# Moving state space constants beside a projection block and loading rows untransformed, in a one-core decoder step

## The chip, the cores and the metric

The kernel runs on one core of a Trainium2 chip. The metric is device time in microseconds (us). Three timed runs stand before the change, and beside them one profiled execution, from which every row below comes.

## The reference, cut to what matters

One inference step of one decoder layer in float32, for 1024 prompt rows and 32 sample rows (8 samples of 4) of width 1024:

```
z  = rmsnorm(x, norm_mix) @ w_in                # [q | k | v | u], 3*768 + 256 columns
q, k = rope(rmsnorm(q)) / 8, rope(rmsnorm(k))   # 12 heads of 64 in 3 groups
attn = dilated window attention of (128,1), (512,4), (2048,16), mixed by a softmax over the groups' lse
y  = S5 state space: a = exp(lam*dt), b = c*B u, h_t = a h_(t-1) + b_t, y = Re(C h) + D u; GLU on gelu(y)
h  = x + [rmsnorm(attn) | rmsnorm(ssm)] @ w_out
h  = h + cross attention(rmsnorm(h), 256 memory rows; sample rows against cached rows) @ w_xo
out = h + ConvFFN(rmsnorm(h))
```

rmsnorm(x, g) is x * rsqrt(mean(x*x) + 1e-6) * g, so the factor of a row and the gain of a column may each be applied to either side of the product with w_in.

## The kernel before

Each product runs as three float32r products (high*high, high*low, low*high) of matrices split into XH, XL (rows, transposed, 128 a tile) and WH, WL (weights, 256 columns a block). ScalarE writes the high half, VectorE subtracts to get the low half. Four stretches follow one another, each a block whose five queues (SyncE for DMA, GpSimd, ScalarE, VectorE, TensorE) are written out by hand; within a queue the order is fixed, between queues there are semaphores.

**block_project** walks 81 steps s: blocks b = 0 to 8 of w_in (for each head group in turn q, k, v; block 2 takes u beside v and is 512 wide), in each the row tiles t = 0 to 8 (tile 8 has 32 rows). In block 0 the rows are made ready too. `prepare(i)` on ScalarE squares and sums tile i (L343) and forms Ln then Exp (L333, L334); on VectorE it refines the root (L89 to L92) and multiplies the tile by factor and gain (L441); TensorE transposes it (L549), ScalarE copies XH (L351), VectorE XL (L448). A step is 24 matmuls (L629), an evacuation by ScalarE (L405, L407), and for q and k blocks a chain for the per-head norm: GpSimd squares (L307), VectorE sums (L458), ScalarE Ln and Exp one step later (L333, L334), GpSimd scales (L286 to L295), VectorE gain and rotation (L466 to L476), TensorE transposes two steps on (L560), ScalarE copies q or k (L383). At the block's start ScalarE asks once for the activation table set `natural_log_exp_and_others` (L327), which has both functions.

Attention of tile a is spread over four steps: scores (L576), mask and maximum on VectorE (L486, L493), exponentials on ScalarE (L363), transposes of the probabilities (L590), their copies on ScalarE (L371) and, where there are 256 keys, on VectorE (L501), the product with V (L605), and the scaling of the result (L509). In a step VectorE does `take_output`, `mask_and_max`, `take_probabilities` in this order. The group with 256 keys in nearly every tile runs beside block 8.

Weights go through one buffer, wstage: SyncE loads it when the split before it is done; ScalarE splits in four pieces of 128x512 (L322), VectorE too (L433).

**block_middle** does the state space layer, the sample rows' attention over cached rows (28 pairs of key tiles, each transposed at L1350 and multiplied at L1363, loads by SyncE into ring slots), and brings everything into XH, XL for the output product. VectorE begins with constants from lam and dt (L1086 to L1135, with two Sin on ScalarE at L952, L953), then the input weights (WBR, WBI), the output table CA; GpSimd doubles a table of unit powers ER, EI from 1 to 128 columns (L870 to L875), then multiplies U by D (L897). VectorE's scans (L1185 to L1202) wait for that table. The Toeplitz parts follow (L1447, DMA to TZ, L1457), y (L1473, L1477), the sample softmax (L1230 to L1245), the mixing weights of the groups (L1254 to L1279), the gates (L1525), and 36 pieces of transposes (L1560) with a high half on ScalarE (L1051) and a low half on VectorE (L1318). The first block of w_out is split in between (L1064, L1333).

**block_dense** multiplies by w_out, the memory weights and w_xq; **block_cross** is cross attention in 16 units, with 64 cached tiles of the samples loaded into an 8-slot ring; the first block of w_xo is split in its unit 14 (L2116, L2186). Then block_dense by w_xo, and the ConvFFN, which the change leaves alone.

Of the kernel before, what the change touches and what calls it, by code (L numbers as in the profile page):

```python
# [13 lines left out]
P = 128  # L14
# [85 lines left out]
def block_project(nc, I, O, S):  # L100
# [12 lines left out]
    MM, TR, SC, OB = bank[0:3], bank[3:5], bank[5:7], bank[7]  # L113
    BLOCKS = 9
# [5 lines left out]
    with ExitStack() as c:  # L120
# [6 lines left out]
        ssq = sb("ssq", [P, 3, TILES])  # L127
        zs = sb("zs", [P, 3, GW])
# [12 lines left out]
        x_ld = [sem(f"x_ld{i}") for i in range(2)]  # L141
        x_sq = sem("x_sq")
        x_rt = sem("x_rt")
        x_n = sem("x_n")
# [29 lines left out]
        zero = sem("zero")  # L174

# [27 lines left out]

        def due(s, after):

            return [a for a in range(G * NT) if start[a] + after == s]
# [17 lines left out]
        def _(sp):  # L224
# [5 lines left out]

            for i in range(TILES):
                if i >= 2:
                    sp.wait_ge(x_tr, 2 * (i - 1))
                src = I["x_prompt"][0, P * i:P * i + P, :] if i < NT else \
                    I["x_sample"].rearrange("b t d -> (b t) d")
                sp.dma_start(xin[:rows(i), i % 2, :], src).then_inc(x_ld[i % 2], 16)
# [5 lines left out]
            lamR, lamI, dt_, Bin = S["ssm_in"]  # L242
# [11 lines left out]
            for s in range(BLOCKS * TILES + 1):  # L254
                b, t = s // TILES, s % TILES
                if s - 1 in k_step:
# [19 lines left out]
        def _(pool):  # L276
            nc.gpsimd.memset(S["eps"][:], EPS).then_inc(zero, 1)
            link = linker(pool, c_pool)

            def scale(q):  # L280
# [4 lines left out]
                sums, r, tmp = (zr[:n, x, q] for x in range(3))  # L285
# [5 lines left out]
                if q >= 4:  # L291
                    pool.wait_ge(z_tr, q - 3)
                    if k_stores[q]:
# [3 lines left out]
                                        per_head(zr[:n, 1, q], n), ALU.mult).then_inc(z_s, 1)  # L297

            for s in range(BLOCKS * TILES):
# [9 lines left out]
                if s in norm_at:  # L309
                    scale(norm_at[s])  # L310

# [4 lines left out]
        def split_weights_act(act, n):  # L316
# [3 lines left out]
            for x in range(CHUNKS):  # L320
                ks = slice(KC * x, KC * x + KC)
                nc.scalar.activation(WH[:, n % 2, ks], wstage[:, ks], ACT.Copy).then_inc(w_hi, 1)  # L322

        @blk.scalar
        def _(act):
# [10 lines left out]
            def prepare(i):  # L336

                if i < TILES:
                    n = rows(i)
                    act.wait_ge(x_ld[i % 2], 16 * (i // 2 + 1))  # L340
                    if i:
                        act.wait_ge(x_sq, i)
                    nc.scalar.activation(junk[:n], xin[:n, i % 2], ACT.Square,  # L343
                                         accum_out=ssq[:n, 0, i:i + 1]).then_inc(x_sq, 1)
                    act.wait_ge(x_sq, i + 1)
                    rsqrt_of_mean(ssq[:n, 0, i:i + 1], ssq[:n, 1, i:i + 1], D).then_inc(x_rt, 1)
                if 0 < i <= TILES:
                    n = rows(i - 1)
                    for half in range(2):
                        act.wait_ge(x_tr, 2 * (i - 1) + half + 1)  # L350
                        nc.scalar.activation(XH[:, 4 * half:4 * half + 4, P * (i - 1):P * (i - 1) + n],  # L351
                                             TR[half][:, 0:4 * P].rearrange("p (k n) -> p k n", k=4)[:, :, :n],
                                             ACT.Copy).then_inc(x_hi, 1)
            prepare(0)
            prepare(1)
            split_weights_act(act, 0)

# [26 lines left out]

            for s in range(LAST):
                b, t = s // TILES, s % TILES
                turn, kind, n = b // 3, b % 3, rows(t)
                if b == 0:
                    prepare(t + 2)
                if b < BLOCKS:  # L390
# [12 lines left out]
                    act.wait_ge(mm, s + 1)  # L403
                    if b == PAIR:
                        nc.scalar.activation(U[:, :, t] if t < NT else US[:, :].rearrange("p (g h) -> p g h", g=16),  # L405
                                             MM[s % 3][:n, WB:2 * WB].rearrange("p (g h) -> p g h", g=16), ACT.Copy)
                    nc.scalar.activation(dst, src, ACT.Copy).then_inc(ev, 1)  # L407
                    if s in take_at:
                        take_q_or_k(take_at[s])
                    if s in norm_at:  # L410
# [3 lines left out]
                        rsqrt_of_mean(zr[:n_q, 0, q], zr[:n_q, 1, q], E).then_inc(z_rt, 1)  # L414
# [9 lines left out]
        def _(dve):  # L424
            link = linker(dve, c_dve)
            dve.wait_ge(tab, 16 * len(S["tables"]))
            link(nc.vector.tensor_scalar(qk_gain[:, 0], qk_gain[:, 0], E ** -0.5, None, ALU.mult))

            def split_weights(n):
                for x in range(CHUNKS):  # L430
                    ks = slice(KC * x, KC * x + KC)
                    dve.wait_ge(w_hi, CHUNKS * n + x + 1)
                    nc.vector.tensor_tensor(WL[:, n % 2, ks], wstage[:, ks], WH[:, n % 2, ks].bitcast(F32),  # L433
                                            ALU.subtract).then_inc(w_lo, 1)

            def prepare(i):
                if i < TILES:
                    n = rows(i)
                    dve.wait_ge(x_rt, i + 1)
# [3 lines left out]
                if 0 < i <= TILES:  # L443
                    n = rows(i - 1)
                    for half in range(2):
                        dve.wait_ge(x_hi, 2 * (i - 1) + half + 1)
                        ks, ts = slice(4 * half, 4 * half + 4), slice(P * (i - 1), P * (i - 1) + n)
                        nc.vector.tensor_tensor(XL[:, ks, ts],  # L448
                                                TR[half][:, 0:4 * P].rearrange("p (k n) -> p k n", k=4)[:, :, :n],
                                                XH[:, ks, ts].bitcast(F32), ALU.subtract).then_inc(x_lo, 1)  # L450
            prepare(0)
            prepare(1)
            split_weights(0)

            def sum_squares(q):
                n = rows(QK[q][1])
                dve.wait_ge(z_sq, q + 1)
                nc.vector.tensor_reduce(zr[:n, 0, q], zsq[:n, q % 2].rearrange("p (h e) -> p h e", h=H),  # L458
# [45 lines left out]
            def take_output(a):  # L504
# [3 lines left out]
                dve.wait_ge(at_pv, a + 1)  # L508
                nc.vector.tensor_tensor(att[:, at].rearrange("p (h e) -> p h e", h=H),  # L509
                                        OB[:, 0:GW].rearrange("p (h e) -> p h e", h=H),  # L510
                                        per_head(rl[:, at], P), ALU.mult).then_inc(at_o, 1)

            for s in range(LAST):
                b, t = s // TILES, s % TILES
                if b == 0:
                    prepare(t + 2)
# [15 lines left out]
        def _(pe):  # L532
# [7 lines left out]
            pe.wait_ge(tab, 16 * len(S["tables"]))  # L540

            def transpose_x(i):
                n = rows(i)
                pe.wait_ge(x_n, i + 1)
# [2362 lines left out]
```

## Time and profile before

| | us |
|---|---|
| three timed runs | 1947.91, 1943.61, 1944.77 |
| median | 1944.77 |
| the profiled execution, its own time | 1944.68 |
| its span, first to last instruction | 1942.8 |
| TensorE busy in the span | 1792.9 (92%) |
| VectorE, ScalarE, GpSimd busy | 960.4, 665.6, 249.0 |
| mean granted clock | 0.962 |

The profiled execution lies 0.1 us from the median, and 1.9 us of it lie outside its span. TensorE's idle time is 150 us. A busy TensorE isn't one at full speed: the granted clock has two levels, 1.2 and 2.4 GHz, and the mean granted clock tells how much of a stretch was at the higher one.

### The profile page before, as it was taken

Reading aid. Unit: us, or ns where it says so; the run is one execution under the profiler, and the core shown is the slowest. Engines: PE = TensorE matmul, PEld = TensorE weight load, DVE = VectorE, ACT = ScalarE, POOL = GpSimd, SP = SyncE. Lnnn points to the kernel's source line nnn. Section 1 sums busy time; section 2 is a strip of 40 time slices with the busy share of each in tenths; the row PEclk is TensorE's granted clock in tenths of the full one; section 3 lists DMA queues with packets and bytes.
Section 4 is the critical chain, followed back from the end, with each engine's and each line's share of the span. In section 5 each row is a group of like instructions: output and inputs, shape, how many; then the busy total and the mean of one; then the engine's idle time right before and its main releaser. Section 6 shows DMA issues by size and latency. Waiting matters only on the chain. (4 is left out here: it accounts for less than half of the span.)

```text
span 1942.8 us, 31346 instructions
## 1 busy us (share of the span) xinstructions
PE 1792.9 (92%) x12419; PEld 1633.8 (84%) x12419; DVE 960.4 (49%) x1929; ACT 665.6 (34%) x1559; POOL 249.0 (13%) x566
## 2 busy tenths in 40 slices
PE   5889999998586998999999989999999999999998
PEld 5888998986354998898678979899899899889996
DVE  5523524646556534653353264545555454454545
ACT  5424324444155323543432054233223223223230
POOL 1511611608221000000000000000000000000000
PEclk9999999998786999999999989999999999999999
DMA  4210110005242532200642112111211112112102
GB/s 151 61 47 32 47 39 26 4 5 158 47 144 85 196 97 77 77 23 27 197 127 74 44 34 56 54 47 34 65 33 56 43 33 66 33 33 66 32 23 90
DMA packets 136239, 125.66 MB, mean 65 GB/s; under 512 B 15722, under 2 KB 128434, under 8 KB 136116
## 3 DMA queue, kind: packets, MB, share of 16 engines
q1 hardware_dynamic: 130500, 109.74, 18.4%
q0 software_dynamic: 5632, 14.44, 2.3%
q8 instruction: 74, 1.21, 0.3%
q14 instruction: 33, 0.27, 0.0%
HBM read 112.79 MB, written 10.70 MB: 64 GB/s over the span
## 5 line engine op out<-in xcount | busy, mean ns | idle before, releaser
L2649 PE MATMUL bank<-XH,WH 128*128 128x352 f32 x1056 | 344.4, 326 | 1.0 <-PEq L1612 1.0
L2649 PE MATMUL bank<-XH,WL 128*128 128x352 f32 x1056 | 342.0, 324 | 0.0
L2649 PE MATMUL bank<-XL,WH 128*128 128x352 f32 x1056 | 341.1, 323 | 0.0
L1969 PE MATMUL bank<-WH,XH 128*128 128x256 f32 x768 | 223.9, 292 | 12.4 <-DVE WL L1836 7.4
L1969 PE MATMUL bank<-WL,XH 128*128 128x256 f32 x768 | 219.5, 286 | 0.0
L629 PE MATMUL bank<-WH,XH 128*128 128x256 f32 (+3 forms) x648 | 212.2, 328 | 7.7 <-DVE WL L433 7.7
L1969 PE MATMUL bank<-WH,XL 128*128 128x256 f32 x768 | 218.5, 285 | 0.0
L2557 DVE TENSOR_TENSOR hres<-hres,bank 128x512 f32<-128x512 f32 (+2 forms) x198 | 135.7, 686 | 158.2 <-PE bank L2682 158.2
L629 PE MATMUL bank<-WL,XH 128*128 128x256 f32 (+3 forms) x648 | 203.7, 314 | 0.0
L629 PE MATMUL bank<-WH,XL 128*128 128x256 f32 (+3 forms) x648 | 203.3, 314 | 0.0
L2649 PEld LDWEIGHTS bank<-XH,WH 128*128 128x128 f32 x1056 | 199.5, 189 | 2.7 <-issue 1.1
L2649 PEld LDWEIGHTS bank<-XL,WH 128*128 128x128 f32 x1056 | 200.0, 189 | 0.4
L2649 PEld LDWEIGHTS bank<-XH,WL 128*128 128x128 f32 x1056 | 199.3, 189 | 0.0
L1969 PEld LDWEIGHTS bank<-WH,XH 128*128 128x128 f32 x768 | 148.4, 193 | 14.0 <-DVE WL L1836 8.1
L2513 DVE SCALAR_TENSOR_TENSOR cv<-UB,pT,cv 128x1072 f32<-128x1072 f32 x44 | 58.7, 1334 | 191.9 <-ACT cv L2460 191.9
L629 PEld LDWEIGHTS bank<-WH,XH 128*128 128x128 f32 (+1 forms) x648 | 139.8, 216 | 11.0 <-issue 8.8
L1969 PEld LDWEIGHTS bank<-WH,XL 128*128 128x128 f32 x768 | 148.6, 193 | 0.0
L1969 PEld LDWEIGHTS bank<-WL,XH 128*128 128x128 f32 x768 | 148.5, 193 | 0.0
L629 PEld LDWEIGHTS bank<-WL,XH 128*128 128x128 f32 (+1 forms) x648 | 140.3, 216 | 1.5
L629 PEld LDWEIGHTS bank<-WH,XL 128*128 128x128 f32 (+1 forms) x648 | 139.6, 215 | 1.7
L2451 ACT ACTIVATE UB<-bank 128x352 f32<-128x352 f32 x88 | 36.1, 463 | 281.0 <-PE bank L2649 281.0
L2682 PE MATMUL bank<-DH,AH 128*128 128x512 f32 x320 | 127.2, 398 | 1.4 <-DVE hres L2557 1.4
(494 smaller groups left out, 3260.0 us busy)
## 6 DMA issues: line engine op xcount, KB each, us to landing
wstage<-w_up SPq DMA_DIRECT2D x44, 512.0 KB, 5.3
ring<-cache_mem_kv SPq DMA_DIRECT2D x64, 256.0 KB, 3.8
dstage<-w_down POOLq DMA_DIRECT2D x22, 512.0 KB, 3.8
wstage<-w_in SPq DMA_DIRECT2D x10, 1024.0 KB, 5.3
ringS<-cache_kv_dil SPq DMA_DIRECT2D x16, 512.0 KB, 6.4
wstage<-w_xkv SPq DMA_DIRECT2D x8, 1024.0 KB, 5.8
ringS<-cache_kv_dil SPq DMA_DIRECT2D x48, 128.0 KB, 2.8
xin<-x_prompt SPq DMA_DIRECT2D x8, 512.0 KB, 3.5
```

The costliest lines, as they stand in the source:

```text
L629: ins = nc.tensor.matmul(out, x, w[:, :, k] if pair else w[:, load % 2, k], start=k == 0 and j == 0, stop=k == KT - 1 and j == 2)
L1969: ins = nc.tensor.matmul(MM[s % 3][:r, 0:WB], x[:, k, cols], w[:, b % 2, k], start=k == 0 and i == 0, stop=k == KT - 1 and i == 2)
L2451: nc.scalar.activation(UB[:, g, 2 + CH * j:2 + CH * j + CH], bank[3 * g + j][:, 0:CH], ACT.Copy)
L2513: nc.vector.scalar_tensor_tensor(cv[:, g], UB[:, g, 1:W - 1], taps(slot, 17, g), cv[:, g], ALU.mult, ALU.add).then_inc(c_dve, 1)
L2557: nc.vector.tensor_tensor(dst, dst, bank[6 + u % 2][:r], ALU.add).then_inc(y, 1)
L2649: ins = nc.tensor.matmul(bank[3 * g + j][:, 0:CH], w[:, slot, k, P * g:P * g + P], x[:, k, CH * j:CH * j + CH], start=k == 0 and i == 0, s ...
L2682: ins = nc.tensor.matmul(out[:r, :], x, w[:, cols], start=s == 0 and i == 0, stop=s == 1 and i == len(terms) - 1)
```

## The change

It has four places.

Start of block_project: the rows are transposed as loaded (three buffers for them rather than two, the first weights asked for before the other tables). The gain of the norm goes into the weights, as the scale of ScalarE's split and as the scalar of VectorE's, now eight pieces of 128x256 each. The factor of a row goes into the evacuation, as a per-partition scale; for the v blocks of the dilated groups it is brought into their order through a small DRAM tensor.

State space constants: the whole of their computation stands in block 2 of block_project, Exp and Sin included, and the table of unit powers up to 64 columns on GpSimd; block_middle does the last doubling.

Order: in block_project `take_probabilities` comes ahead of `mask_and_max` on VectorE. In block_middle the weights' transposes come earlier, keys are divided otherwise (0-2, 2-4, 4-6, 6-16, 16-24, 24-28), the three sums of squares stand after the scans, the first four pieces of the last part are taken ahead of the root, and GpSimd makes the low half of the first w_out block.

block_cross: the second half of the cached tiles uses 12 slots (the four of kTx too), and the split of w_xo's first block moves from unit 14 to behind unit 15.

```diff
@@ block_project
-        zr = sb("zr", [P, 3, len(QK), H])
+        zr = sb("zr", [P, 3, 8, H])
-            xin = early.enter_context(nc.sbuf_tensor("xin", [P, 2, D], F32))
+            xin = early.enter_context(nc.sbuf_tensor("xin", [P, XB, D], F32))      # XB = 3
+        def row_factor(s):
+            b, t = s // TILES, s % TILES
+            order = GROUPS[b // 3] if b % 3 == 2 and t < NT else 0
+            return (r_dil[:, order - 1] if order else ssq[:, 1])[:rows(t), t:t + 1]
@@ sync
+            sp.dma_start(S["ident"][:], I["c_ident"]).then_inc(id_ld, 16)
             for i in range(TILES):
-                if i >= 2:
-                    sp.wait_ge(x_tr, 2 * (i - 1))
+                if i >= XB:
+                    sp.wait_ge(x_tr, 2 * (i - XB + 1))
+                    sp.wait_ge(x_sq, i - XB + 1)
...
                 if i == 0:
+                    sp.dma_start(gain[:], I["norm_mix"][0].rearrange("(k p) -> p k", p=P),
+                                 allow_slow_non_contiguous=True).then_inc(g_ld, 16)
+                    load_weights(0)
+                if i == 2:
                     for dst, src in S["tables"]:
                         sp.dma_start(dst, src).then_inc(tab, 16)
-                if i in (1, 4):
-                    load_weights(i // 4)
+                if i == 4:
+                    load_weights(1)
...
+                if (b, t) == (1, 1):
+                    sp.wait_ge(x_r, TILES)
+                    (store ssq[:, 1] to rowf, wait, load r_dil twice)
@@ gpsimd
+                if (b, t) == (PAIR, 3):
+                    unit_powers()                # 3 squarings, then doubling from 1 to 64 columns
@@ scalar
-            for x in range(CHUNKS):
-                ks = slice(KC * x, KC * x + KC)
-                nc.scalar.activation(WH[:, n % 2, ks], wstage[:, ks], ACT.Copy).then_inc(w_hi, 1)
+            for k in range(KT):
+                ins = nc.scalar.activation(WH[:, n % 2, k], wstage[:, k], ACT.Copy, scale=gain[:, k:k + 1])
+                if k % KC == KC - 1:
+                    ins.then_inc(w_hi, 1)
...
+            take_rows(0)
+            act.wait_ge(g_ld, 16)
             split_weights_act(act, 0)
+            mean_square(0)
...
+            def step_sizes():
+                act.wait_ge(S["ld_lam"], S["n_lam"])
+                nc.scalar.activation(dt_[:], dt_[:], ACT.Exp).then_inc(p_dt, 1)
+            def magnitude_and_angle():
+                act.wait_ge(p_exp, 1)
+                nc.scalar.activation(sm[:, 1], sm[:, 0], ACT.Exp).then_inc(p_exp, 1)
+                act.wait_ge(p_ang, 1)
+                nc.scalar.activation(sm[:, 16], sm[:, 5], ACT.Sin).then_inc(p_sin, 1)
+                nc.scalar.activation(sm[:, 17], sm[:, 4], ACT.Sin).then_inc(p_sin, 1)
             for s in range(LAST):
                 b, t = s // TILES, s % TILES
-                if b == 0:
-                    prepare(t + 2)
+                if (b, t) == (PAIR, 0):
+                    step_sizes()
+                if (b, t) == (PAIR, 2):
+                    magnitude_and_angle()
+                if b == 0 and t < NT:
+                    take_rows(t + 1)
...
+                    if b == 0:
+                        act.wait_ge(x_r, t + 1)
+                    if s == 2 * TILES:
+                        act.wait_ge(r_ld, 32)
-                    nc.scalar.activation(dst, src, ACT.Copy).then_inc(ev, 1)
+                    nc.scalar.activation(dst, src, ACT.Copy, scale=row_factor(s)).then_inc(ev, 1)
...
+                if b == 0 and t < NT:
+                    mean_square(t + 1)
@@ vector
-                    refine_rsqrt(nc, link, ssq[:n, 0, i:i + 1], ssq[:n, 1, i:i + 1], ssq[:n, 2, i:i + 1], D)
-                    nc.vector.scalar_tensor_tensor(xin[:n, i % 2], xin[:n, i % 2], ssq[:n, 1, i:i + 1],
-                                                   gain_bc[:n], ALU.mult, ALU.mult).then_inc(x_n, 1)
...
                 if b == 0:
-                    prepare(t + 2)
+                    finish_factor(t)             # the four small operations of refine_rsqrt
+                    if t < NT:
+                        take_rest(t + 1)         # XL
+                if (b, t) == (PAIR, 1):
+                    decay_and_angle()
+                if (b, t) == (PAIR, 3):
+                    powers()
+                if (b, t) == (PAIR, 5):
+                    input_weights()
...
                 for a in due(s, 3):
                     take_output(a)
+                for a in due(s, 2):
+                    take_probabilities(a)
                 for a in due(s, 0):
                     mask_and_max(a)
-                for a in due(s, 2):
-                    take_probabilities(a)
@@ block_middle
 sync
-            load_ring(0, 3)
+            load_ring(0, 2)
...
+            load_ring(RING, 8)
+            sp.wait_ge(e_tab, 1)
             sp.dma_start(gain_bc[:, 0:AW], I["attn_out_norm"][0].partition_broadcast(P)).then_inc(ld_g, 16)
             sp.dma_start(gain_bc[:, AW:D], I["ssm_out_norm"][0].partition_broadcast(P)).then_inc(ld_g, 16)
-            load_ring(RING, 20)
+            load_ring(8, 18)
             sp.wait_ge(tz, 4)
...
-            load_ring(20, 24 + RING)
+            load_ring(18, 24 + RING)
 gpsimd
-            (3 squarings of the unit step, then doubling of ER, EI from 1 to 128 columns)
+            (8 operations on 128x512: ER, EI [0:64] copied, [64:128] made from them, scratch in CA) -> e_tab
...
+            pool.wait_ge(S["w_first_hi"], 1)
+            nc.gpsimd.tensor_tensor(S["WL"][:, 0], S["wstage"][:], S["WH"][:, 0].bitcast(F32), ALU.subtract)\
+                .then_inc(S["w_first"], 1)
 scalar
             nc.scalar.preload_act_table_set("natural_log_exp_and_others")
-            act.wait_ge(ld_lam, S["n_lam"])
-            nc.scalar.activation(dt_[:], dt_[:], ACT.Exp).then_inc(p_dt, 1)
             nc.scalar.activation(st[:, :, 0], lsum[:], ACT.Ln).then_inc(lnp, 1)
-            (Exp, Sin, Sin)
...
-            take_keys(22, KPAIRS)
+            squares(1)
+            take_keys(24, KPAIRS)
+            squares(2)
 vector
-            (decay and angle, powers, input weights: L1086 to L1135)
...
             dve.wait_ge(t_c, 1)
+            dve.wait_ge(e_tab, 1)
...
-            sum_squares(0)                       # ahead of the scans
...
-            sum_squares(1)
-            sum_squares(2)
+            for g in range(G):
+                sum_squares(g)
...
+            for k in range(EARLY):               # 4, ahead of the root
+                take_rest(k)
             dve.wait_ge(so_r, 1)
...
-            nc.vector.tensor_tensor(S["WL"][:, 0], S["wstage"][:], S["WH"][:, 0].bitcast(F32), ALU.subtract)\
-                .then_inc(S["w_first"], 1)
@@ block_cross
-    slot = [n % RING if n < 2 * NL - LATE else 4 + n % 4 for n in range(2 * NL)]
+    WIDE = RING + SLOTS
+    slot = [n % RING if n < NL else (n - NL) % WIDE for n in range(2 * NL)]
...
-                if v == NU - 2:
-                    act.wait_ge(S["w_next"], 32)
-                    act.wait_ge(vp, NL - LATE)
-                    nc.scalar.activation(WH[:, 0], wstage[:], ACT.Copy).then_inc(S["x_hi"], 1)
             act.wait_ge(vp, NL)
             nc.scalar.activation(Ps[:], SB[:, 2 * P:4 * P], ACT.Copy).then_inc(so_c, 1)
+            act.wait_ge(S["w_next"], 32)
+            nc.scalar.activation(WH[:, 0], wstage[:], ACT.Copy).then_inc(S["x_hi"], 1)
             take_output(NU - 1)
```

## Rows read from the trace of the kernel before

**Rows 1.** The page's part 2: TensorE and its granted clock in 40 slices.

```profile
PE   5889999998586998999999989999999999999998
...
PEclk9999999998786999999999989999999999999999
```

**Rows 2.** TensorE's waits, 0 to 480 us: waited for, total us, times, longest.

```profile
PE bank L549 <- DVE xin L441: 13.3, 1, 13.3
...
PE bank L605 <- DVE PT L501: 6.6, 6, 2.7
```

**Rows 3.** TensorE's waits, 470 to 640 us, same columns.

```profile
PE bank L1447 <- DVE R L1188: 16.3, 1, 16.3
PE bank L1560 <- DVE XL L1318: 14.0, 6, 10.2
PE bank L1457 <- DMA TZ<-R: 7.0, 1, 7.0
```

**Rows 4.** Stretches of the span: length, busy us and instructions of each engine, clock.

```profile
core 0: us, PE busy (x) PEld busy (x) DVE busy (x) ACT busy (x) POOL busy (x), PEclk, DMA share, GB/s
18.34:73.97 55.63, 43.06 (x287) 40.00 (x285) 35.71 (x96) 27.88 (x75) 17.47 (x50) 0.88 0.32 91
...
206.96:244.39 37.43, 37.17 (x315) 36.40 (x314) 21.96 (x71) 14.74 (x52) 29.42 (x84) 1.00 0.11 36
341.35:372.57 31.22, 31.08 (x263) 30.52 (x262) 18.72 (x60) 12.61 (x44) 24.31 (x70) 1.00 0.00 1
401.41:430.97 29.56, 26.43 (x220) 24.40 (x218) 14.85 (x24) 11.77 (x41) 0.00 (x0) 1.00 0.01 1
439.55:624.47 184.92, 125.11 (x1527) 84.74 (x1525) 118.60 (x269) 84.80 (x180) 70.54 (x98) 0.79 0.37 103
```

**Rows 5.** Timeline at the start: start us, us, instruction; and the page's weight loads.

```profile
4.76 0.43 SPq L228 DMA_DIRECT2D wstage<-w_in  x1
...
18.34 0.56 PE L629 MATMUL bank<-WH,XH 128*128 128x256 f32 x1
...
wstage<-w_in SPq DMA_DIRECT2D x10, 1024.0 KB, 5.3
```

**Rows 6.** VectorE's groups, 0 to 75 us: busy us, mean ns, idle before.

```profile
L441 DVE SCALAR_TENSOR_TENSOR xin<-xin,ssq,gain_bc 128x1024 f32<-128x1024 f32 (+1 forms) x9 | 11.9, 1327 | 0.3
```

**Rows 7.** Timeline of ScalarE in one step of block 3.

```profile
210.18 0.39 ACT L407 ACTIVATE zs<-bank 128x256 f32<-128x256 f32 x1 [1.99 <-PE bank L629]
210.46 0.38 ACT L383 ACTIVATE qT<-bank 128x256 f32<-128x256 f32 x1
210.72 0.30 ACT L333 ACTIVATE zr<-zr,eps 128x4 f32<-128x4 f32 x1
211.05 0.21 ACT L334 ACTIVATE zr<-zr 128x4 f32<-128x4 f32 x1
```

**Rows 8.** Timeline of ScalarE in the middle: table loads and what follows them.

```profile
444.13 1.28 ACT L952 ACT_TABLE_LOAD   x1
...
546.68 1.28 ACT L999 ACT_TABLE_LOAD   x1
547.97 0.21 ACT L999 ACTIVATE sc<-sc 128x3 f32<-128x3 f32 x1
548.20 1.28 ACT L1001 ACT_TABLE_LOAD   x1
...
561.32 1.28 ACT L1012 ACT_TABLE_LOAD   x1
```

**Rows 9.** Timeline of VectorE in the middle's first half.

```profile
443.70 0.17 DVE L1086 TENSOR_TENSOR sm<-lamR,dt_ 128x8 f32<-128x8 f32 x1 [0.32 <-ACT dt_ L947]
...
454.77 1.23 DVE L1073 TENSOR_TENSOR WBR<-PR,BpR 128x1024 f32<-128x1024 f32 x1
...
484.36 0.69 DVE L1185 TENSOR_TENSOR XR<-ER,bank 128x512 f32<-128x512 f32 x1 [9.04 <-POOL EI L875]
...
488.85 2.83 DVE L1073 TENSOR_TENSOR XI<-XI,R 128x512 f32<-128x512 f32 x1
```

**Rows 10.** Timeline of GpSimd there: last doubling's operations, then U by D.

```profile
481.82 1.28 POOL L874 TENSOR_TENSOR ER<-XR 128x512 f32<-128x512 f32 x1
...
486.02 5.11 POOL L897 TENSOR_TENSOR U<-U,Dbc 128x1024 f32<-128x1024 f32 x2
```

**Rows 11.** Timeline of ScalarE and VectorE at the middle's last part.

```profile
596.46 1.15 ACT L1051 ACTIVATE XH<-bank 128x256 fp32r<-128x256 f32 x4
...
600.58 1.40 DVE L1318 TENSOR_TENSOR XL<-bank,XH 128x256 fp32r<-128x256 f32 x4
614.06 2.28 DVE L1333 TENSOR_TENSOR WL<-wstage,WH 128x2048 fp32r<-128x2048 f32 x1
```

**Rows 12.** TensorE's waits, 640 us to the end.

```profile
PE bank L2259 <- DMA ring<-cache_mem_kv: 2.3, 1, 2.3
PE bank L2224 <- DVE PT L2144: 2.2, 2, 1.6
```

More of the change, by code:

```diff
@@ L127, in block_project @@
         ssq = sb("ssq", [P, 3, TILES])
+        r_dil = sb("r_dil", [P, 2, NT])
+        gain = sb("gain", [P, KT])
         zs = sb("zs", [P, 3, GW])
@@ L139, in block_project @@
         PT = sb("PT", [P, 2, 2 * H, P])
-        x_ld = [sem(f"x_ld{i}") for i in range(2)]
+        x_ld = [sem(f"x_ld{i}") for i in range(XB)]
         x_sq = sem("x_sq")
         x_rt = sem("x_rt")
-        x_n = sem("x_n")
+        x_r = sem("x_r")
+        r_st, r_ld = sem("r_st"), sem("r_ld")
+        id_ld, g_ld = sem("id_ld"), sem("g_ld")
         x_tr = sem("x_tr")
@@ L283, in scale @@
                 pool.wait_ge(z_rt, q + 1)
-                sums, r, tmp = (zr[:n, x, q] for x in range(3))
+                sums, r, tmp = (zr[:n, x, q % 8] for x in range(3))
                 link(nc.gpsimd.tensor_scalar(tmp, sums, -0.5 / E, -0.5 * EPS, ALU.mult, ALU.add))
@@ L425, in _, with split_weights @@
             link = linker(dve, c_dve)
+            def split_weights(n):
+                for x in range(CHUNKS):
+                    dve.wait_ge(w_hi, CHUNKS * n + x + 1)
+                    for k in range(KC * x, KC * x + KC):
+                        ins = nc.vector.scalar_tensor_tensor(WL[:, n % 2, k], wstage[:, k], gain[:, k:k + 1],
+                                                             WH[:, n % 2, k].bitcast(F32), ALU.mult, ALU.subtract)
+                    ins.then_inc(w_lo, 1)
@@ new lines, in take_rest @@
+            def take_rest(i):
+                n = rows(i)
+                for half in range(2):
+                    dve.wait_ge(x_hi, 2 * i + half + 1)
+                    ks, ts = slice(4 * half, 4 * half + 4), slice(P * i, P * i + n)
+                    nc.vector.tensor_tensor(XL[:, ks, ts],
+                                            TR[half][:, 0:4 * P].rearrange("p (k n) -> p k n", k=4)[:, :, :n],
+                                            XH[:, ks, ts].bitcast(F32), ALU.subtract).then_inc(x_lo, 1)
@@ new lines, in finish_factor @@
+            def finish_factor(i):
+                n = rows(i)
+                dve.wait_ge(x_rt, i + 1)
+                sums, r, tmp = (ssq[:n, x, i:i + 1] for x in range(3))
+                link(nc.vector.tensor_scalar(tmp, sums, -0.5 / D, -0.5 * EPS, ALU.mult, ALU.add))
+                link(nc.vector.tensor_tensor(tmp, tmp, r, ALU.mult))
+                link(nc.vector.tensor_tensor(tmp, tmp, r, ALU.mult))
+                nc.vector.scalar_tensor_tensor(r, tmp, 1.5, r, ALU.add, ALU.mult).then_inc(x_r, 1)
@@ L426, in _ @@
+            take_rest(0)
+            dve.wait_ge(g_ld, 16)
+            split_weights(0)
             dve.wait_ge(tab, 16 * len(S["tables"]))
             link(nc.vector.tensor_scalar(qk_gain[:, 0], qk_gain[:, 0], E ** -0.5, None, ALU.mult))
[L429 to L434, printed above, removed]
@@ L964, in _, with take_weights @@
             take_u(3)
-            squares(0)
-            take_keys(0, 4)
+            take_keys(0, 2)
+            def take_weights(q):
+                act.wait_ge(t_b, q + 1)
+                nc.scalar.activation((WBR, WBI)[q // 2][:, 4 * (q % 2):4 * (q % 2) + 4],
+                                     QB[q][:].rearrange("p (g n) -> p g n", g=4), ACT.Copy).then_inc(wb, 1)
+            for q in range(3):
+                take_weights(q)
+            take_keys(2, 4)
             act.wait_ge(us_p, 1)
@@ L1064, in _ @@
             nc.scalar.activation(S["WH"][:, 0], S["wstage"][:], ACT.Copy).then_inc(S["w_first_hi"], 1)
-            for k in range(22, len(work)):
+            for k in range(23, len(work)):
                 take_head(k)
@@ L1204, in _ @@
                     dve.wait_ge(h_ok, 1)
-            sum_squares(1)
-            sum_squares(2)
+            for g in range(G):
+                sum_squares(g)
             dve.wait_ge(s_rd, 3)
@@ L1304, in _, with take_rest @@
                     .then_inc(so_m, 1)
+            def take_rest(k):
+                dve.wait_ge(x_h, k + 1)
+                dst, n = place(XL, work[k])
+                hi, _ = place(XH, work[k])
+                src = mix_bank(k)[:, 0:2 * P].rearrange("p (k n) -> p k n", k=2)[:, :, :n]
+                nc.vector.tensor_tensor(dst, src, hi.bitcast(F32), ALU.subtract).then_inc(x_l, 1)
+            for k in range(EARLY):
+                take_rest(k)
             dve.wait_ge(so_r, 1)
@@ L1401, in _, with transpose_weights @@
             transpose_u(3)
-            keys(0, 4)
+            keys(0, 2)
+            def transpose_weights(q):
+                for g in range(4):
+                    ins = nc.tensor.transpose(QB[q][:, P * g:P * g + P], (WBR, WBI)[q // 2][:, 4 * (q % 2) + g], ident[:])
+                ins.then_inc(t_b, 1)
+            pe.wait_ge(u_t, 4)
+            pe.wait_ge(bb, 1)
+            for q in range(3):
+                transpose_weights(q)
+            keys(2, 4)
             pe.wait_ge(ld_us, 16 * DT)
@@ L2012, in block_cross @@
         ss = sb("ss6", [P, 4])
-        r_ld = [sem(f"r_ld{i}") for i in range(RING)]
+        r_ld = [sem(f"r_ld{i}") for i in range(WIDE)]
         zero, qz = sem("zero"), sem("qz")
@@ L2030, in filled, with cached @@
             return x.rearrange("p b (h n) -> p b h n", h=X)[:, :, :, 0:DT]
+        def cached(n):
+            return ring[:, slot[n]] if slot[n] < RING else kTx[:, slot[n] - RING]
         def out_place(Xt, u):
```

375 lines of the change are left out of this document (189 added, 186 removed).

## The prediction, made before the changed kernel was run

> **What bounds the kernel now.** I read the 40 slices first [rows 1]. TensorE is at 8 or 9 tenths nearly everywhere; the holes are the first slice (5) and the 10th to 13th (8, 5, 8, 6), which are the middle, and the clock row dips only in these four. So the kernel is bound by TensorE, which idles 150 us of 1942.8: 18.3 before the first product [rows 5], 12.6 between 18.34 and 73.97 (block 0) and 59.8 in the middle [rows 4]. In the norm steps 33 to 44 TensorE is all but full, 37.17 of 37.43 us, and ScalarE has 14.74; in 60 to 69 it is 31.08 of 31.22 and 12.61 [rows 4]. Then TensorE's waits by releaser: the head waits for the first normalised tile (13.3), attention for VectorE's copy of PT (6.6 in six) [rows 2]; the middle for the scans' R (16.3), for XL (14.0) and for TZ (7.0) [rows 3]; later parts for the ring (2.3) and PT (2.2) [rows 12]. A gain must come from these waits; a loss needs an engine that passes TensorE.
>
> **Head.** Removed: nine L441 on VectorE, 11.9 us [rows 6], and the path norm, then transpose. The transposes need only a loaded tile, so the 13.3 us wait [rows 2] is replaced by one for the weights. They are asked for at 4.76 [rows 5], eighth on SyncE's queue; now fourth, four issues of 0.43 earlier (-2), and nothing of tables or broadcast gain (0.5 MB) goes ahead of their 1 MB: 5.3 us to landing by the page's row, where 18.34 - 4.76 leaves 13.6 for landing and split. Landing near 8, first quarter split and copied (about 2), transposes and tile copies beside it: first matmul at about 12.5, -5.8 (bounds -2, the issues alone, and -8). After it block 0 is a chain of ScalarE, GpSimd and VectorE: 55.6 us for nine steps, 6.2 each, TensorE busy 43.1 [rows 4]. Of the 1.33 us that leave VectorE per step half lies on that chain (bounds: none, all): 9 x 0.66 = -6. Added: ScalarE scales by a pointer. No row has a Copy with one; L333 with its bias pointer takes 0.30 beside L334 without, 0.21 [rows 7]: 0 to 0.09 each, I take 0.09. Eight split pieces for four cost about +0.8 on ScalarE, and each evacuation waits for the row's factor (x_r), behind which stand Ln and Exp of the chain: +3 together in block 0. Head: -9 (-4 to -13). The store and two loads for r_dil are on SyncE at step 10 and needed at step 18; behind them queue only stores of k, eight steps ahead of use. Nothing.
>
> **Constants in block 2.** Steps there are 512 columns wide, twice a norm step's 3.10 us of TensorE, and have no norm: VectorE's chain of 443.70 to 454.77, 11 us [rows 9], is spread over six steps, and GpSimd's small operations too lie beside 6.2 us of products a step. Cost 0; without that cover, 11.
>
> **Order of VectorE.** PT ahead of mask and maximum takes VectorE's mask work off the path to L605. The waits listed are 6.6 us [rows 2]; mask and maximum stand ahead of PT in each of them, and explain those in block 8 and part of the other two. I take -5.5, bounds 0 and -8.2 (with L560's).
>
> **Middle.** The path was: 11 us of constants, table doubled on GpSimd until 484.3, scans from 484.36 after 9.04 us of idle VectorE [rows 9], and then VectorE slowed beside GpSimd's L897 (128x512 in 2.83 against 0.69 [rows 9, 10]). Now eight operations of 128x512 at 1.28 [rows 10] are 10.2 us, so it is there by 460 even if they start ten us into the middle, and the scans start when their products are there: these wait for transposes and keys that TensorE has in its order ahead of them, near 475 as I place it (-9; bounds 0 and -19, from 484.36 to 465, VectorE's constants gone and nothing else late), and run some 3.5 faster. L1447's 16.3 wait [rows 3] is filled with keys, which are only moved, so the gain is the part of it that TensorE can't fill again later. TZ's 7.0 goes too, since the TZ stores no longer queue on SyncE behind ring loads up to 19. Against: SyncE waits for e_tab, and the gain rows and eleven ring loads stand behind it (ring tiles late by about 5 us); three sums and squares stand ahead of the sample softmax, +5 to 6 on its chain. Tail: four pieces ahead of the root take 4 us of XL's 14.0 [rows 3], and WL (2.28 on VectorE [rows 11]) goes to GpSimd: 2048 columns by L897's 5.11 for 2 x 1024 [rows 10] are 5.1 us, needed only after the last transposes, so hidden; if it slows VectorE's 0.35 us pieces [rows 11] as L897 did, +4. With Sin gone from the middle the set asked for at its start stays: the loads at L952, L999, L1001 and L1012 [rows 8] go, two of them off the softmax (-2.6), which then waits for its DMA round trip. Together -18: 13 of scans, TZ and softmax, 5 of tail; bounds -6 (tail and one wait) and -24.
>
> **Cross.** Twelve slots remove the ring wait, 2.3, and about 1.5 of half-clock products behind it; PT's 2.2 goes [rows 12]. The split of w_xo now stands after the last unit: ScalarE and VectorE need some 2 us each there, hidden in part by take_output: +1.5. Sum -4.5 (0 to -6).
>
> **Table loads.** This is the step that costs. Block 2 now calls Sin at step 20, after the one request for the joint Ln and Exp set (L327). While that set is in, a norm is Ln and Exp with no load between [rows 7]. After a Sin the trace of before shows otherwise: L999 loads 1.28 us for Ln, the next instruction begins 0.01 later, and then L1001 loads 1.28 again for Exp [rows 8]. The same would hold for the 36 norms after step 20: 72 loads, 92 us of ScalarE. Blocks 3, 4, 6 and 7 with no attention give 23 pure steps (33 to 44, 60 to 70). ScalarE there has 14.74 / 12 = 1.23 us, 1.05 counting overlap [rows 4, 7]; with 2.56 of loads, 0.09 to 0.18 of pointers and 0.1 of waits about 3.9, against TensorE's 37.17 / 12 = 3.10. So ScalarE sets these steps: +0.8 x 23 = +18. Two of them also split weights (+3 each, +6); the four norm steps with attention, whose steps are longer, +3; +1 of clock. Sum +28. Ends: 0 (no loads) and +56 (rival B).
>
> A rule stands beside it. The Trainium skill, "ScalarE: Activation LUTs", section "What ACT_TABLE_LOAD costs", gives a load about 1283 ns and a drain of about 1380 ns after it. The row's 1.28 agrees; the 0.01 us that follow L999's load do not [rows 8]. By the page's drain the sum would have 72 x 1.38 = 99 us more; by the row, none.
>
> **Sum.** -9 - 5.5 - 18 - 4.5 + 28 = -9. The profiled execution took 1944.68, 0.1 under the median: 1936.
>
> **Rivals.** *A, the joint set comes back.* If what follows Sin is one load of the joint set, or the set of Ln holds Exp, one load is hidden in block 2 and the other four gains stay: 1944.7 - 37 = 1908. For: the request's name is a set with both, and [rows 7] run on it. Against: [rows 8], where Exp right after Ln loads again. A sentence of the Trainium skill speaks for it ("ScalarE: Activation LUTs", section on table sets): ln then exp is one load, since natural_log_exp_and_others has both; rows 8 contradict it, and by it the time is this rival's.
>
> *B, slower: the clock follows the idle.* In the steps bound by ScalarE TensorE idles 0.8 of 3.9 us. If its clock falls to the lower level there, 24 matmuls that take 3.10 at the higher one take up to 6.2, and about 5.1 with the weight loads that overlap: 1.2 above the 3.9, x 23 = +28 more: 1964. It decides where the mean clock of steps 33 to 44 goes below about 0.8. For: in block 0, 12.6 idle of 55.6 goes with 0.88, in the middle 0.79. Against: in 401.41 to 430.97 TensorE idles 3.13 of 29.56 in gaps under a microsecond at clock 1.00 [rows 4].
>
> *C, the middle gives little.* If the cache tiles' DMAs bound the middle, and not the scans (DMA share 0.37 [rows 4], and SyncE now stops for e_tab), the waits come back as waits for ring tiles, and the softmax, 5 us later, takes the tail's gain: middle -6, 1948. For: 16.3 us of wait is filled with keys that must come 12 us sooner. Against: no wait of TensorE for ring tiles among the large ones now [rows 3].
>
> **How the numbers follow.** Forecast 0.50, own range 1926 to 1946 (each gain at its lower half to its upper, table loads 20 to 34); A 0.14; B 0.20; C 0.16. A measurement tells about 0.2%, 3.9 us, from no change. Faster (below 1940.9): of the forecast 0.37, A 0.14, of C 0.02: 0.53. Same: 0.09 of the forecast, 0.08 of C, 0.02 of B: 0.19. Slower: the rest, 0.28. The range goes from A to just short of B's middle: 1908 to 1962; outside remain half of A and half of B.
>
> **What would show it.** The first L629 at 12 to 13 and no VectorE operation of 1.33 us in block 0. No VectorE idle for EI, scans from about 475, L1447's wait under 5. No load at the middle's Ln or Exp; L605's wait for PT under 2; L2259's for the ring gone. ScalarE's groups: 72 table loads between steps 28 and 72, steps 33 to 44 in 46 to 48 us rather than 37.4, TensorE waiting there for the evacuation. Wrong would be: one load after Sin, or none (A); steps 33 to 44 above 55 at a clock under 0.8 (B); a wait for ring tiles of over 8 us in the middle (C); or ScalarE's time under 3.1 a step for another reason, such as a norm without its own loads.

## The result and the profile after

| | before | after |
|---|---|---|
| median of 4 runs, us | 1946.03 | 1964.01 (1962.04 to 1969.19) |
| ratio, 95% interval | | 1.0093 [1.0076, 1.0110] |
| span of the profiled execution | 1942.8 | 1962.5 |
| ScalarE busy | 665.6 | 774.6 |
| mean granted clock | 0.962 | 0.954 |

The change made the kernel 0.9% slower where 0.4% faster was forecast. TensorE's row and its clock in the 40 slices of the changed kernel's page, beside [rows 1]: the first slice is fuller, there are new holes in the 4th, 5th, 8th and 9th, and the clock dips in the 8th and 9th too.

```profile
PE   6898799879867889899898989999999999999998
...
PEclk9999999889787899999999989999999999999999
```

ScalarE's groups in the changed kernel (line, operation, count | busy us, mean ns | idle before): behind the two Sin, while TensorE is at steps 28 to 73, the Ln of a norm (L402) and its Exp (L403) each bring a load of an activation table, 72 in all, 92.4 us.

```profile
L402 ACT ACT_TABLE_LOAD x36 | 46.2, 1283 | 0.6
L403 ACT ACT_TABLE_LOAD x36 | 46.2, 1283 | 0.6
...
L402 ACT ACTIVATE zr<-zr,eps 128x4 f32<-128x4 f32 (+1 forms) x54 | 15.9, 294 | 2.7 <-DVE zr L553 2.3
```

Where the time went in the two traces. A step of block_project begins with its first product, and so does each later stretch, with two exceptions: the middle is counted from the end of the last product by w_in, and the stretch to the ConvFFN from the end of cross attention's last product.

| stretch | before | after | difference |
|---|---|---|---|
| to step 0 | 18.3 | 12.9 | -5.4 |
| steps 0 to 8 | 55.6 | 50.7 | -4.9 |
| steps 9 to 26 | 101.1 | 104.7 | +3.6 |
| 27 to 32 (attention) | 31.9 | 37.2 | +5.3 |
| 33 to 44 | 37.4 | 51.2 | +13.8 |
| 45 to 54 | 67.7 | 66.7 | -1.0 |
| 55 to 59 (attention) | 29.3 | 37.9 | +8.6 |
| 60 to 69 | 31.2 | 42.3 | +11.0 |
| 70 to 74 (attention) | 28.8 | 38.5 | +9.6 |
| 75 to 80 (attention, no norm) | 38.1 | 34.0 | -4.1 |
| middle | 184.9 | 172.1 | -12.8 |
| products to cross attention | 293.4 | 293.0 | -0.3 |
| cross attention | 117.4 | 112.4 | -4.9 |
| to the ConvFFN | 121.2 | 123.8 | +2.6 |
| ConvFFN and end | 786.5 | 785.1 | -1.4 |

Five of these stretches as windows of the changed kernel (columns as in [rows 4]): steps 0 to 8, steps 33 to 44, 60 to 69, 75 to 80, middle.

```profile
12.95:63.64 50.69, 40.02 (x286) 37.34 (x285) 27.81 (x99) 32.90 (x89) 16.14 (x50) 0.90 0.35 98
...
205.49:256.69 51.20, 41.05 (x315) 38.74 (x314) 23.31 (x75) 48.49 (x81) 24.93 (x79) 0.93 0.07 24
...
361.28:403.54 42.26, 33.84 (x264) 31.95 (x261) 19.78 (x63) 40.78 (x68) 20.70 (x66) 0.96 0.00 1
...
442.01:476.02 34.01, 34.01 (x293) 32.47 (x292) 16.80 (x29) 13.88 (x43) 0.00 (x0) 1.00 0.02 6
476.02:648.16 172.14, 131.44 (x1525) 90.24 (x1525) 110.92 (x213) 77.32 (x170) 54.66 (x47) 0.77 0.40 111
```

In steps 33 to 44 and 60 to 69 ScalarE is busy 48.49 of 51.20 us and 40.78 of 42.26: the bound has moved to it, where [rows 4] had 14.74 of 37.43. The timeline of one such step, beside [rows 7], has a load ahead of each function (last row: the next step's first load begins 3.76 us after this one's):

```profile
221.90 1.28 ACT L402 ACT_TABLE_LOAD   x1
223.20 0.30 ACT L402 ACTIVATE zr<-zr,eps 32x4 f32<-32x4 f32 x1
223.51 1.28 ACT L403 ACT_TABLE_LOAD   x1
224.80 0.20 ACT L403 ACTIVATE zr<-zr 32x4 f32<-32x4 f32 x1
224.92 0.45 ACT L497 ACTIVATE zs<-bank,ssq 128x256 f32<-128x256 f32 x1
225.27 0.37 ACT L453 ACTIVATE qT<-bank 128x256 f32<-128x256 f32 x1
225.66 1.28 ACT L402 ACT_TABLE_LOAD   x1
```

### The profile page after: what moved, and what is told of

It reads as the page before. It is cut to its first block and busy times, and to the rows that moved or that the text cites. A ratio compares the mean times of both kernels' runs of the same rounds, so it can differ in the third digit from the quotient of the medians.

```text
span 1962.5 us, 31508 instructions
## 1 busy us (share of the span) xinstructions
PE 1810.8 (92%) x12419; PEld 1647.8 (84%) x12419; DVE 958.2 (49%) x1959; ACT 774.6 (39%) x1667; POOL 238.4 (12%) x569
## 3 DMA queue, kind: packets, MB, share of 16 engines
q1 hardware_dynamic: 133620, 109.23, 18.3%
```

## The experiments

The kernel before was timed again beside each group of experiments (median 1948.48 beside E1 to E4, 1948.28 beside E5 to E8, 1943.03 beside E9 and E10, and 1946.03 beside the changed kernel). Across groups the medians can be some us apart for this reason alone, so the difference by the ratios to the kernel before is given too, as us of 1946.

**E1: the joint set asked for again.** The changed kernel with one line, after the two Sin:

```diff
                 nc.scalar.activation(sm[:, 17], sm[:, 4], ACT.Sin).then_inc(p_sin, 1)
+                nc.scalar.preload_act_table_set("natural_log_exp_and_others")
```

> The changed kernel with one more line: right after its two Sin in block 2 ScalarE asks again for the joint set of Ln and Exp. Theory L (the loss is the 72 table loads, by all they set off): the stretches from the first step of block 3 to the end of block 7 give back what they lost, 24.9 us in the steps without attention and 24.8 in those with it; ScalarE shows no load between steps 28 and 72; about 1964 - 49 = 1915. Theory P (part of that loss is something else: evacuations scaled by a pointer, splits in eight pieces, banks held longer): only the forecast's +28 goes, 1936, and steps 33 to 44 stay above 38 us.

Measured 1916.22 us, ratio 0.9836 [0.9822, 0.9850]: 47.8 us under the changed kernel (50 by the ratios), for one added load. ScalarE's groups of this kernel show single loads in block_project, for the request at the start, for Sin and for the request behind it:

```profile
L396 ACT ACT_TABLE_LOAD x1 | 1.3, 1283 | 1.0 <-PEq L3013 1.0
L463 ACT ACT_TABLE_LOAD x1 | 1.3, 1283 | 0.0
L465 ACT ACT_TABLE_LOAD x1 | 1.3, 1283 | 0.0
```

Its windows of steps 33 to 44 and of the middle (the profiled execution of E1 is the fastest of its five, 4.9 under their median, so its trace flatters it a little):

```profile
199.46:237.37 37.91, 37.27 (x315) 36.42 (x314) 23.95 (x81) 16.79 (x56) 28.75 (x83) 1.00 0.10 33
427.97:593.36 165.39, 124.70 (x1525) 83.88 (x1525) 109.84 (x213) 77.25 (x170) 54.72 (x47) 0.82 0.42 115
```

Against the changed kernel the five stretches (steps 27 to 32, 33 to 44, 55 to 59, 60 to 69, 70 to 74) give back 6.1, 13.3, 9.7, 10.4 and 8.6 us, 48.0 together: 23.7 in the two with norms alone, 24.3 in the three with attention. Theory L holds; theory P's 1936 is far off, and 37.91 against 37.43 before (38.5 in E4) is all that pointers and eight pieces cost in twelve steps.

**E2: the loads alone.** The kernel before, with an unused Sin in step 20:

```diff
+                if (b, t) == (PAIR, 2):
+                    nc.scalar.activation(junk[:, 0:1], S["eps"][:], ACT.Sin)
```

> The kernel before with one Sin on a 128x1 tile added on ScalarE in step 20, its result unused: the table loads alone. Theory L: every norm of steps 28 to 45 and 55 to 72 loads twice, and the time goes up by 45 to 50 us, to about 1994, half of it in the steps that have attention. Theory P: +28, about 1974.

Measured 1995.40, ratio 1.0244 [1.0227, 1.0262]: +46.9 us. The page of this kernel has the same 72 loads, under the lines of the kernel before:

```profile
L333 ACT ACT_TABLE_LOAD x36 | 46.2, 1283 | 0.7
L334 ACT ACT_TABLE_LOAD x36 | 46.2, 1283 | 0.7
```

By the same stretches the trace has 49.3 us more than that of the kernel before, 27.7 of them in the three with attention, as theory L says. So one Sin at a place where ScalarE is idle costs 47 us, without anything else of the change.

**E3: take_output ahead of the norm.** The changed kernel, loads and all, on VectorE:

```diff
-                if s in norm_at:
-                    norm_and_rotate(norm_at[s])
                 for a in due(s, 3):
                     take_output(a)
+                if s in norm_at:
+                    norm_and_rotate(norm_at[s])
```

> The changed kernel, table loads and all, with take_output ahead of norm_and_rotate on VectorE in each step. Theory Q (in steps with attention the loads cost through a queue: VectorE waits for the norm that stands behind both loads, and the scaling of the last attention result stands behind that wait, and TensorE's next product with V behind that): the two waits of TensorE for att, 6.8 us between 170 and 257, go, and of the 24.8 us lost in those steps about 10 come back, 1954. Theory S (there too ScalarE's busy time sets the pace): no change, 1964.

Measured 1954.47, ratio 1.0025 [1.0010, 1.0041]: 9.5 us under the changed kernel by the medians, 9.9 by the two spans and 13 by the ratios, with every load in place. The queue it removed, in step 29 of the changed kernel (timelines of ScalarE, GpSimd, VectorE, TensorE, put one below the other; idle time and what ended it in brackets):

```profile
177.13 1.28 ACT L402 ACT_TABLE_LOAD   x1
178.43 0.30 ACT L402 ACTIVATE zr<-zr,eps 128x4 f32<-128x4 f32 x1
178.75 1.28 ACT L403 ACT_TABLE_LOAD   x1
180.04 0.20 ACT L403 ACTIVATE zr<-zr 128x4 f32<-128x4 f32 x1
```

```profile
180.33 0.19 POOL L352 TENSOR_SCALAR zr<-zr 128x4 f32<-128x4 f32 x1 [2.52 <-ACT zr L403]
...
181.76 0.61 POOL L361 TENSOR_TENSOR zn<-zs,zr 128x256 f32<-128x256 f32 x1
```

```profile
182.41 0.42 DVE L561 TENSOR_TENSOR zn<-zn,qk_gain 128x256 f32<-128x256 f32 x1 [4.15 <-POOL zn L361]
...
183.98 0.42 DVE L606 TENSOR_TENSOR att<-bank,rl 128x256 f32<-128x256 f32 x1
```

```profile
184.55 1.94 PE L779 MATMUL bank<-V,PT 128*128 128x64 f32 x8 [3.10 <-DVE att L606]
```

Read upward from the product with V: it waited 3.10 us for L606 to empty its bank; L606 stands in VectorE's order behind L561, before which VectorE was idle for 4.15 us; L561 waited for GpSimd, and GpSimd for the Exp behind both loads. ScalarE is busy 23.32 of 32.06 us in steps 28 to 32, so not full; the loads cost here as latency of a chain. TensorE's longest waits in steps 27 to 44 (170 to 257 us of the changed kernel, 168 to 254 of E3):

```profile
PE bank L734 <- DVE zn L571: 10.2, 8, 4.0
PE bank L779 <- DVE att L606: 6.8, 2, 3.7
```

```profile
PE bank L734 <- DVE zn L571: 10.0, 9, 4.0
PE bank L803 <- DVE WL L522: 2.7, 1, 2.7
```

The wait for att is gone, as theory Q says; steps 27 to 32 take 33.3 us for 37.2, and 55 to 59 take 32.4 for 37.9. Steps 70 to 74 stay at 37.8, for 38.5. Together the three stretches give back 10.1, so the queue explains about 10 of the 24.3 us; the waits that are left are for zn (the norm's own chain) and for PT and Sm, and they weren't taken apart.

**E4: the middle undone.** The changed kernel with the constants back in the middle and block_middle as before (no short diff: it is the change's middle part reversed).

> The changed kernel with the state space constants back in the middle and the whole middle as before: head, order and cross remain, and there is no Sin in block 2. Theory L: no table loads in the norms, so -7 for the head, -5 for the order, -2 for the cross part: about 1932, and 17 above the kernel with the set asked for again, which is then what the middle is worth. Rival: the middle is worth 12.8 as the two traces' stages say: 1928. If head, order and cross gave all they were forecast to (-19): 1927.

Measured 1929.06, ratio 0.9904 [0.9888, 0.9920]: 12.8 above E1, which is what the middle is worth by the medians (16.3 by the two traces, 181.7 for 165.4). Head, order and cross together are 19.4 under the kernel before by the medians and 17.3 by the spans. That is near the forecast's -19 for the three, but 3.2 of the 17.3 lie in the middle (181.7 for 184.9), whose code is the same in both kernels, so it is no proof of the three terms.

**E5 and E6: order and cross undone.** E1 with the mask ahead of PT again (the change's swap reversed), and E1 with the old block_cross.

> The kernel with the set asked for again (1916), mask and maximum put back ahead of the copy of PT on VectorE. Theory: the order is worth 5.5, of it 3.8 to 4.2 in steps 75 to 80: 1921.5. Rival: TensorE's waits on PT are replaced by waits on the mask, and only block 8's 4.2 is there and part given back in the turns: 1918.

> The kernel with the set asked for again (1916), with block_cross as it was before. Theory (stage table: cross itself -5.2, the product by w_xo behind it +2.3): 2.9 slower, 1919. Rival, the forecast's own term: 4.5 slower, 1920.5. Third: the later split of w_xo costs all that the twelve slots give, 1916.

E5: 1921.60, ratio 0.9867 [0.9848, 0.9887], 5.4 over E1 (6.0 by the ratios), and its interval just touches E1's; in its trace 4.3 more stand in steps 75 to 80. E6: 1918.05, ratio 0.9849 [0.9825, 0.9873], 1.8 over E1 (2.5 by the ratios), and its interval takes in E1's ratio, so by the times the two can't be told apart. By the stages E6 has 6.8 more in cross attention and 2.3 less behind it; TensorE's idle time ahead of the first product by w_xo is 3.1 us in E1 and 2.0 in E6. That this is the late split of w_xo fits the order of the code, but the profile names no releaser for it.

**E7: ring tiles ahead of TZ.** E1 with

```diff
-            load_ring(8, 18)
+            load_ring(8, 20)
...
-            load_ring(18, 24 + RING)
+            load_ring(20, 24 + RING)
```

> The kernel with the set asked for again (1916), with loads 18 and 19 of the sample cache ahead of the eight stores to TZ on SyncE instead of behind them. Theory (TensorE's 5.3 us wait for a ring tile at 490.85 comes from SyncE's queue: the load stood behind the stores, which stood behind ScalarE's R): the wait goes, the stores end 1 to 2 us later, net -4 at the sample softmax if that follows the keys: 1912. Rival (the tile's DMA time or the slots bound it, or the softmax chain swallows it): 1916, the wait moves to TZ or to PmS.

Measured 1910.87, ratio 0.9813 [0.9790, 0.9837], 5.3 under E1 (4.5 by the ratios), with intervals that overlap. Waits of TensorE in the middle, E1 and E7:

```profile
PE bank L1600 <- DVE PmS L1355: 7.7, 1, 7.7
PE bank L1459 <- DMA ringS<-cache_kv_dil: 5.3, 1, 5.3
PE bank L1622 <- DMA ringS<-cache_kv_dil: 4.8, 2, 4.5
```

```profile
PE bank L1600 <- DVE PmS L1355: 7.7, 1, 7.7
PE bank L1622 <- DMA ringS<-cache_kv_dil: 3.3, 3, 2.4
...
PE bank L1459 <- DMA ringS<-cache_kv_dil: 3.0, 1, 3.0
PE bank L1571 <- DMA TZ<-R: 2.8, 1, 2.8
```

The wait of 5.3 at this tile is gone, so the queue was its cause; the 3.0 at the same line is that of another tile, some 35 us earlier. 2.8 come back as a wait for TZ, as the rival said in part.

**E8: squares earlier.** E1 with ScalarE's order in the middle:

```diff
-            take_keys(16, 24)
+            take_keys(16, 20)
+            squares(1)
+            take_keys(20, 24)
...
-            squares(1)
-            take_keys(24, KPAIRS)
-            squares(2)
+            squares(2)
+            take_keys(24, KPAIRS)
```

> The kernel with the set asked for again (1916), with ScalarE's squares of groups 1 and 2 taken one stop earlier (amid keys 16 to 24, and ahead of keys 24 to 28), so that VectorE's sums end before the sample scores do. Theory (VectorE's last sum of 2.29 us and what follows it stand ahead of the sample softmax: TensorE waits 7.7 for PmS): the softmax starts 3 to 5 us earlier, PmS wait 4 or less, 1912. Rival (the waits for the last cache tiles behind it, 4.5 us, take the gain): 1915 to 1916.

Measured 1907.11, ratio 0.9782 [0.9758, 0.9806]: 9.1 under E1 (10.5 by the ratios). PmS falls from 7.7 to 2.4:

```profile
PE bank L1460 <- DMA ringS<-cache_kv_dil: 8.5, 2, 4.7
...
PE bank L1601 <- DVE PmS L1356: 2.4, 1, 2.4
```

The middle of its profiled execution is only 1.1 us shorter than E1's (164.3 for 165.4): TensorE is idle 5.2 us less, though the wait for ring tiles rose to 8.5, and busy 4.1 us more for the same products, at a granted clock of 0.80 for 0.82. Its span is 1.9 under E1's, its median 9.1. That the sums stood in the way is shown, how much of the 9 is theirs is not.

**E9 and E10: both together, and E3's order beside them.**

> The set asked for again, with both changes to the middle: squares earlier (alone 1907) and loads 18 and 19 ahead of the TZ stores (alone 1911). Theory (the two waits stand one behind the other: for a ring tile, then for PmS, and with the squares early the ring tiles set the end): together they save about 2 more than the squares alone, 1905. If they were independent: 1916 - 9 - 5 = 1902. If both feed the same wait: 1907.

> As the one before, with take_output ahead of norm_and_rotate on VectorE too. With the table loads that order saved 9.5 of 1964. Theory Q (it paid by taking the wait for the loads' norm off the attention's path; with no loads there is no such wait): within 1.5 of the kernel without it. Rival (it pays by itself: the waits for zn and att remain in the attention steps): 3 or more faster.

E9: 1906.10, ratio 0.9802 [0.9785, 0.9819]. E10: 1902.92, ratio 0.9785 [0.9769, 0.9802]. In E9's trace the middle is 157.9 us, 7.5 under E1, yet its ratio isn't under E8's. E10 is 3.2 under E9, which is what the rival expected and not theory Q, but the intervals overlap, and the two spans are the same within 0.2: the three stretches with attention are 3.2 shorter in E10 and its middle is 3.6 longer. So whether E3's order pays without the loads stays open. E8, E9 and E10 can't be told apart; all are about 2% faster than the kernel before, and faster than E1.

## Why the prediction was wrong

The signs of its steps were right; the sum failed by one term, the price of the table loads in the steps that have attention.

**Head.** Forecast -9 (first product at 12.5). Measured first product at 12.95, and -10.3 at the end of block 0; then +3.6 in blocks 1 and 2, where the text had counted nothing: -6.7. Steps 10 and 14 are 1.1 and 1.0 longer, and in each TensorE waits for VectorE's rotated zn (0.9 and 1.2 us), where the trace of before shows no such wait; why zn is late was not tested. Step 18 is 1.0 longer too, 8.38 us for 7.36, but TensorE is busy all through it in both kernels: it waits for no r_dil, and the granted clock is 0.68 for 0.80. The pointer's price, taken as 0.09 from [rows 7], is 0.08: the evacuation's mean over blocks 1 to 8 is 468 ns for 384.

**Constants.** Forecast 0; steps 19 to 26 are 0.2 us longer in sum. The constants are hidden, and their cost lies in the table set that they leave behind on ScalarE.

**Order.** Forecast -5.5, E5 shows 5.4 by its median, 4.3 of it placed by its trace.

**Middle.** Forecast -18. -12.8 in the changed kernel, -19.5 in E1's trace. The code and TensorE's idle time (40.7 us) are the same in both, but the granted clock is 0.77 in one and 0.82 in the other, and TensorE busy 131.44 against 124.70 us: the 6.7 us between them are the clock. What lowered it is not shown. With the loads ahead of it the same middle took 172.1 and 170.7 us (changed kernel, E3), without them 165.4, 166.3 and 167.3 (E1, E5, E6); the old middle took 184.9 without and 184.3 with them (E2). The scans begin 37.4 us into the middle for 44.8, -7.4 where -9 was taken; what holds them is no more the table EI [rows 9] but their own products:

```profile
513.41 0.69 DVE L1294 TENSOR_TENSOR XR<-ER,bank 128x512 f32<-128x512 f32 x1 [3.22 <-PE bank L1547]
```

No load is left at the middle's Ln and Exp, as forecast. The two things that the forecast named as against it were both there: SyncE's queue, with the ring load behind the TZ stores (a wait of 5.89 us), and the sums ahead of the softmax (7.67).

**Cross.** Forecast -4.5: cross attention alone gave 4.9, but the stretch behind it, into which the split moved, is 2.6 longer, for which +1.5 stood in the sum; net -2.3.

**Table loads.** Forecast +28, E1 and E2 measure 47.8 (50 by the ratios) and 46.9. This is the step that failed, and within it one line: "the four norm steps with attention, whose steps are longer, +3; +1 of clock". For norms alone, splits included, it took 24; E1 gives 23.7 back in the two stretches there, and a step without a split took 3.8 to 4.0 us for the 3.9 forecast. In the steps with attention (27 to 32, 55 to 59, 70 to 74) stand 12 of the 36 loading norms, not four, and they took 24.3: 2.0 a norm where 0.75 was taken. They were priced by ScalarE's busy share, which still had room, and not by the chain on which both loads lie: Ln, Exp, GpSimd, VectorE's norm, and in VectorE's queue behind it the attention's result. E3 shows that queue, worth about 10. The other 14 stay open as to their path; the granted clock is lower there too, 0.84, 0.82 and 0.87 in steps 28 to 32, 55 to 59 and 70 to 74, for 0.93, 0.94 and 1.00 before.

**The rivals.** A (one load of the joint set after Sin) is wrong for this code and is what E1 makes true: 1916 for its 1908. The sentence cited for it from the Trainium skill, "ScalarE: Activation LUTs", section on table sets, holds in these traces only while the set asked for by name is in (E1); after a Sin with no new request each Ln and each Exp loads (E2, 72 loads). B gave 1964 by another road: steps 33 to 44 took 51.2 us at clock 0.93, not over 55 at under 0.8; the number is a coincidence. C names the right waits (a ring tile, 5.9 us, and the softmax, 7.7), and a middle of -12.8 lies between it and the forecast.

By the measured terms: -6.7 - 5.4 - 12.8 - 2.3 + 47.8 = +20.6, for +19.7 between the two spans. The terms come in part from traces and in part from medians, so part of that closeness is luck: head, order and cross are 14.4 here, and 17.3 to 19.4 in E4.

## What to carry to other kernels

A request for an activation table set held here only until a function outside it ran (Sin, the one that was tried): after such a function, ask again, and count the loads in the trace, by number as well as by time. Price what is added to an engine in two ways, by its busy share and by the chain it stands in; where another queue waits for its result with more work behind that wait, the addition can cost most of its length on an engine that has room. Here ScalarE was busy 44% of the steps with attention, and 12 norms' loads, 30.8 us, cost 24.3. A side effect of a few hundred nanoseconds of moved work can be larger than the move's gain; here one line turned +0.9% into -1.6%.

## What the runs showed of the hardware that was not expected

The same products with the same idle time can differ by the granted clock alone: the middle of the changed kernel and that of E1 both leave TensorE idle for 40.7 us and differ by 6.7 us, all of it busy time, at 0.77 against 0.82.

GpSimd and VectorE slow one another. One of GpSimd's last two operations on the table, which began beside VectorE's work, took 2.17 us, and the next, with VectorE idle, 1.31. Of two like products of VectorE, the one beside GpSimd's U by D (L1054, 496.29 to 503.09) took 3.39, the other, beside a memset of GpSimd, 1.36:

```profile
491.18 2.17 POOL L1046 TENSOR_TENSOR ER<-CA 128x512 f32<-128x512 f32 x1
493.29 1.31 POOL L1047 TENSOR_TENSOR EI<-CA 128x512 f32<-128x512 f32 x1
```

```profile
494.70 1.36 DVE L1229 TENSOR_TENSOR CA<-PR,CI_ 128x1152 f32<-128x1152 f32 x1 [2.52 <-POOL EI L1047]
...
500.92 3.39 DVE L1229 TENSOR_TENSOR CA<-PR,CI_ 128x1152 f32<-128x1152 f32 x1
```

In the kernel before, small operations of GpSimd fared worst: one of 128x32 beside VectorE's 128x1024 products took twice as long as one of 128x256, eight times its size, with VectorE idle. Spans on GpSimd are rough, and no run changed this, but it suggests why the table of [rows 9] came so late:

```profile
458.58 1.31 POOL L872 TENSOR_TENSOR XI<-ER,EI 128x32 f32<-128x32 f32 x1
...
475.47 0.62 POOL L873 TENSOR_TENSOR XI<-EI,ER 128x256 f32<-128x256 f32 x1
```
